# TensorE's expert loop in eight rounds of one expert with one code copy, in place of four rounds of a pair with two

## The reference

```python
for i in range(DEPTH):                      # DEPTH = 2
    h = x * (1.0 + sc1) + sh1
    if i % 2 == 0:
        y, s = deltanet_mixer(h, ...)
    else:
        y = pool_mixer(h, ...)
    x = layer_norm(ALPHA * x + g1 * y, ...)
    h = x * (1.0 + sc2) + sh2
    if i % 2 == 0:
        y = swiglu(h, w_gu, w_down)
    else:
        y = moe_swiglu(h, router_w, w_gu, w_down)
    x = layer_norm(ALPHA * x + g2 * y, ...)
```

```python
def moe_swiglu(h, router_w, w_gu, w_down):
    probs = softmax(h @ router_w)
    top_p, top_i = lax.top_k(probs, 2)          # 2 of 8 experts for each token
    gates = ...                                 # the two shares, renormalised
    y = 0
    for e in range(8):                          # w_gu[e] is (1024, 2816), w_down[e] (1408, 1024)
        y = y + gates[..., e:e + 1] * swiglu(h, w_gu[e], w_down[e])
```

## Time and profile before

| | |
|---|---|
| median of 3 runs | 1996.92 us (1995.87 to 2001.87) |
| profiled execution, its own time | 1996.99 us |
| its span, first to last instruction | 1995.4 us |
| TensorE busy | 95% |
| VectorE busy | 56% |
| ScalarE busy | 38% |
| GpSimd busy | 22% |
| mean granted TensorE clock | 0.984 |
| DMA | 321.58 MB, 161 GB/s on average |
| instruction queues | 175 packets with 2.87 MB, 64 with 0.52 MB |

### The profile page before, as it was taken

The page is one execution under the profiler, slowest core; times in us unless marked ns, Lnnn a source line. Parts: engine busy times, 40 slices in busy tenths (PEclk is TensorE's granted clock), DMA queues, the critical chain, the costliest instruction groups (busy, mean ns, idle before and its releaser), DMA issues. The chain is left out here.

```text
span 1995.4 us, 39790 instructions
## 1 busy us (share of the span) xinstructions
PE 1901.1 (95%) x14649; PEld 1550.1 (78%) x14650; DVE 1118.7 (56%) x1771; ACT 754.5 (38%) x1299; POOL 444.7 (22%) x370
## 2 busy tenths in 40 slices
PE   7899999999999999999999998899999999999994
PEld 5888888888886478887778876788887787787882
DVE  4676777677675653223222367665558557554346
ACT  4533442442341122221222203565547547553332
POOL 0245334425422222121111243200000000000015
PEclk9899999999999999999999999999999999999998
DMA  8233234224235352243323624886669669764354
GB/s 279 96 121 122 71 119 142 81 90 151 91 102 173 113 175 93 90 134 116 106 77 100 216 73 158 319 286 194 200 213 320 232 207 321 253 206 162 99 185 158
DMA packets 185238, 321.58 MB, mean 161 GB/s; under 512 B 26303, under 2 KB 77399, under 8 KB 184999
## 3 DMA queue, kind: packets, MB, share of 16 engines
q1 hardware_dynamic: 170567, 287.05, 43.6%
q0 software_dynamic: 8304, 28.84, 4.1%
q10 hardware_dynamic: 6128, 2.30, 0.4%
HBM read 285.45 MB, written 32.67 MB: 159 GB/s over the span
## 5 line engine op out<-in xcount | busy, mean ns | idle before, releaser
L1387 PE MATMUL pp<-whi,xTh 128*128 128x512 f32 (+1 forms) x1152 | 442.3, 384 | 14.8 <-issue 6.6
L1389 PE MATMUL pp<-wlo,xTh 128*128 128x512 f32 (+1 forms) x1152 | 431.0, 374 | 0.0
L1388 PE MATMUL pp<-whi,xTl 128*128 128x512 f32 (+1 forms) x1152 | 430.1, 373 | 0.0
L2144 ACT ACTIVATE whi<-raw_halves 128x1024 fp32r<-128x1024 f32 (+1 forms) x256 | 245.2, 977 | 110.5 <-PE pp L1389 97.2
L1387 PEld LDWEIGHTS pp<-whi,xTh 128*128 128x128 f32 x1152 | 218.1, 189 | 55.0 <-issue 11.0
L1389 PEld LDWEIGHTS pp<-wlo,xTh 128*128 128x128 f32 x1152 | 217.6, 189 | 38.7
L1388 PEld LDWEIGHTS pp<-whi,xTl 128*128 128x128 f32 x1152 | 218.5, 190 | 35.0
L2798 DVE TENSOR_TENSOR wlo<-raw_halves,whi 128x1024 fp32r<-128x1024 f32 (+1 forms) x142 | 165.1, 1163 | 102.1 <-ACT whi L2144 82.4
L1387 PE MATMUL pp<-whi,hTh 128*128 128x512 f32 x503 | 202.4, 402 | 4.7 <-DVE ybuf L2750 2.3
L2807 DVE TENSOR_TENSOR wlo<-raw_halves,whi 128x1024 fp32r<-128x1024 f32 (+1 forms) x142 | 156.8, 1104 | 71.8 <-ACT whi L2144 61.9
L1389 PE MATMUL pp<-wlo,hTh 128*128 128x512 f32 x503 | 196.5, 391 | 0.0
(11 more groups left out here) (369 smaller groups left out, 3302.2 us busy)
## 6 DMA issues: line engine op xcount, KB each, us to landing
raw_halves<-in_moe_w_gu SPq DMA_DIRECT2D x320, 256.0 KB, 4.3
wring<-in_ada_w SPq DMA_DIRECT2D x80, 512.0 KB, 4.7
raw_halves<-in_moe_w_down SPq DMA_DIRECT2D x160, 256.0 KB, 3.4
wring<-in_ffn_w_gu SPq DMA_DIRECT2D x80, 256.0 KB, 2.9
wring<-in_dn_w_in SPq DMA_DIRECT2D x124, 128.0 KB, 2.6
wring<-in_ffn_w_down SPq DMA_DIRECT2D x40, 256.0 KB, 3.0
expert_in<-zeros SPq DMA_DIRECT2D x36, 256.0 KB, 3.3
wring<-in_ada_first SPq DMA_DIRECT2D x32, 256.0 KB, 5.7
```

The costliest lines, as they stand in the source:

```text
L1387: pe.matmul(out, hi[:, c0 + c, tt], wh, start=(first and c == 0), stop=False)
L1388: pe.matmul(out, lo[:, c0 + c, tt], wh, start=False, stop=False)
L1389: mm = pe.matmul(out, hi[:, c0 + c, tt], wl, start=False, stop=(last and c == nk - 1))
L2144: act.activation(whi[:, hs, 0:nk, 0:w], raw_half(l, k, s)[:, 0:nk, 0:w], ACT.Copy)\
```

## The change

TensorE's loop over pairs of experts becomes a loop over experts. The body holds one expert, whose number is the loop's own register. No matmul, wait or transfer is added or taken away, and the other engines' code stays.

```diff
                 if l:
                     rn, rc = expert_counts(pe, n0)
-                    with nc.Fori(0, 4, engines=[pe.engine], hint_back_edge=True) as pair:
-                        for i in range(2):
-                            n, c = this_expert(pe, rn, rc)
-                            n2 = expert(2 * pair + i, n, c)
-                            next_expert(pe, rn, rc, n, n2)
+                    with nc.Fori(0, 8, engines=[pe.engine], hint_back_edge=True) as e:
+                        n, c = this_expert(pe, rn, rc)
+                        n2 = expert(e, n, c)
+                        next_expert(pe, rn, rc, n, n2)
                 else:
                     for e in range(2):
                         expert(e, T, T * e)
```

## The result

The changed kernel took 2008.4 us, the median of 7 runs (2002.8 to 2012.48); the kernel before took 1998.94 us on the same chip (7 runs, 1993.36 to 2001.87). The ratio is 1.005 [1.0036, 1.0064]: slower by 7.2 to 12.8 us, some 10 us in the middle. Predicted were 8.5 us more, and 2005.4 us. The profiled execution took 2009.4 us with a span of 2007.9 us, against 1996.99 and 1995.4 before.

What follows compares the result with a forecast made beforehand. TensorE, busy 95% of the span, was taken as the bound, stopped by fetches of its own code. Terms 5.0 + 0.8 + 0 + 0 + 2.7 + 0 = 8.5 us on 1996.9 gave 2005.4 us; range 1998.5 to 2014.0.

Steps and rivals of the forecast that it cites:

- Expert 0 to 1: New back edge behind one-tile expert 0: target late by 3.2 us plus 1.8 us for the clock, 5.0 us.
- Experts 3 to 4 and 5 to 6: Existing one-tile edges: matmuls last 3.15 us after entry, not 3.57, so 0.4 us more each, 0.8 in all.
- Two-tile edges: Edges 1 to 2, 2 to 3, 4 to 5: 5.4 us of cover against 5.1, so 0; upper end 2.7 us.
- Expert 6 to 7: Edge whose next first matmul is already 1.26 us late for xTl: 6.1 us of cover, so 0.
- Experts 3 and 5 on the first copy's borders: Both experts move to the first copy's block borders and lose 1.35 us each, 2.7 in all; ends 0 and 2.7.
- step 6: Next code block behind each edge comes under queued matmuls: 0; upper end 1.5 us each for experts 3 and 5.
- (a): All edges stop TensorE, two-tile ones too, as the hint is armed too late: say 2013 us; chance 0.16.
- Rival (b): No measurable change: target after 4.6 us at expert 0's edge, borders not to blame; +1.9 us, 1998.8; chance 0.24.
- Rival (c): Faster: ten blocks stay on the chip between rounds, so code waits end; -12.0 us, 1984.9; chance 0.06.

## Why the prediction was right, step by step

The direction, the size and the places came out: +8.5 us forecast, 7.2 to 12.8 measured. Of the 3 us between 2005.4 and 2008.4, 2 are the base (1998.94 in these runs, 1996.9 in the profile I had) and 1 is the sum. In the profiled executions, where the terms can be measured one by one, they come to 10.0 us (6.6 + 1.2 + 2.2) against 8.5, and the spans differ by 12.5.

1. *Expert 0 to 1.* Forecast 3.2 + 1.8 = 5.0, measured 3.8 + 2.8 = 6.6. The mechanism held; both terms were too small. The target came 6.2 us after entry (1311.9 to 1318.1), and I took 5.9, which was the better of two records; that is half of the missing 0.6 us. The other half is cover: without the gap the next matmul would have stood at 1314.75, 2.85 us after entry and not 3.15. The branch of 4.7 us lies just above the 3 to 4.5 I had named. The clock's part I had from an expert behind a gap of 2.62 us, and this gap is 3.65 us. The run with idle matmuls has the same delay and no fall of the clock.
2. *Experts 3 to 4 and 5 to 6.* Forecast 0.4 each; measured 0.7 and 0.5. Here the clock's part did not grow: expert 4 took 95.6 us in both kernels. So the size of the gap alone does not give the clock's price.
3. *Two-tile edges.* Forecast 0 at 1 to 2, 2 to 3 and 4 to 5, and no gap stands there. The target came 3.5, 3.4 and 4.0 us after entry, not 4.6: the 4.6 was an upper bound from a branch that did not have to wait. The choice between 4.6 and 5.9 by DMA load was right in kind, and the run with a quarter of the weights shows the load as the cause.
4. *Expert 6 to 7.* Forecast 0; the branch took 377 ns, and the wait for xTl stayed at 1.26 us.
5. *Experts 3 and 5 on the first copy's borders.* Forecast 2.7 for both; measured 2.2, of which 0.41 belongs to step 6. The waits inside these experts, the first in expert 3, the second in expert 5 of the changed kernel:

```profile
PE pp L1387 <- issue: 1.7, 2, 1.0
...
PE pp L1387 <- issue: 2.7, 3, 1.6
```

Expert 5 went to all of expert 0's 53.7 us, expert 3 only halfway. With a quarter of the weights, on the same borders, these waits are gone, so the weight traffic is shown as a cause. The step took the place of the borders as the cause of the difference, and that is not shown. Experts 3 and 5 run the same code on the same borders and still wait 1.7 and 2.7 us (2.3 without the 0.41 of step 6). The kernels with 64 and 192 instructions ahead of the loop, whose borders lie elsewhere under the same traffic, have 1.8 and 1.7 us, and 2.6 and 1.0 (with 0.9 more in expert 5 that the profile lays to DVE). In the written-out loop expert 3 has 3.6 us. Two experts on the same borders thus differ by 0.1 to 1.6 us, against the 1.35 us forecast for each, so the size that came out here is in part luck.
6. *The next block behind each edge.* Forecast 0. One of them, 3652 ns after edge 4 to 5, opened 0.41 us. The others (2.2 and 2.5 us after the edges 2 to 3 and 0 to 1) opened none.

Of the rivals, (a) is refuted for this kernel by the two-tile edges. It is real, though: the kernel without the hint is this case, and its 2020 us lie above the 2013 that I gave it, since there the one-tile edges lose 1.7 to 2.2 us more as well. Rival (b) asked for 4.6 us under load; 6.0 to 6.2 were measured at all three one-tile edges. Rival (c) is refuted by the blocks: the instruction queue over expert 2 of the changed kernel, which ran the same copy as the expert before it:

```profile
q8 instruction: 11, 0.18, 0.7%
```

Eleven blocks for the whole of expert 2, of a body that had just run: nothing of it stayed on the chip.

## What to carry to other kernels

A loop on a busy engine costs, at each back edge, what the target's code comes late: the time from the entry into the branch's block to the target (here 3.4 to 4.0 us, under full weight traffic 6.0 to 6.2), less the time from that entry to the end of the last matmul ahead of the branch. So short rounds under heavy DMA pay and long ones do not, and rolling a loop up further adds such edges while it saves no fetch as long as the body doesn't stay on the chip. Where the code fits, write the loop out; where it doesn't, keep the back-edge hint, look in the trace at when the branch's block is entered, and move it with skipped code only after finding the border.

## What the hardware showed beyond that

- The place of a block border is worth more than this change was. The same executed work took 2002.6, 2004.3, 2008.4, 2015.6 and 2028.0 us with 70, 64, 0, 192 and 140 skipped instructions (70 and 140 inside the expert, 64 and 192 ahead of the loop; 2002.6 is a single run). A comparison of two TensorE codes of different length has this in it.
- A gap on TensorE can be paid twice. A gap of 3.65 us was followed by 5.6 us at a granted clock of 0.50, which cost 2.8 us; 1.9 us of idle matmuls within the gap kept it at 1.00.
- Fetching code shares the DMA with the weights: a block that takes 6.2 us from entry to target at a DMA share of 0.98 takes under 4 us when a quarter of the weights is loaded. The transfer itself takes 1.0 us in both; what shrinks is the wait for its start, 3.7 us against 1.5.
- The profile blamed code waits on DVE in places (2.12 us on wlo in the run with 64), as in the earlier trace rows. The loop branch's duration is the safer row.
- Not tried: the written-out loop with idle matmuls in its one-tile experts, and, for the kernel before, an order of experts in which no one-tile expert precedes one of its three edges.
